# Attention softmax: one reciprocal for two heads, and sink logits that stay in a column of four buffers

## What is computed

```python
s = jnp.where(valid, s + alibi, -jnp.inf)
sink_logit = jnp.broadcast_to(sink.astype(jnp.float32).reshape(Hkv, rep, 1, 1), ...)
p = jax.nn.softmax(jnp.concatenate([s, sink_logit], axis=-1), axis=-1)[..., :-1]
o = jnp.einsum('bngrqk,bnkgd->bnqgrd', p, vb)
```

## Time and profile before

| what | value |
|---|---|
| median of three runs | 731.63 us (731.01 to 731.79) |
| the profiled execution | 729.93 us |
| its span in the profile | 728.1 us |
| TensorE busy | 703.9 us, 97% of the span |
| VectorE busy | 507.8 us, 70% |
| ScalarE busy | 389.6 us, 54% |
| GpSimd busy | 322.6 us, 44% |
| chain that ended last | TensorE 86%, DMA 5%, VectorE 4% |
| line 1544 (sink copies) | 16, 3.4 us in all |
| line 1554 in 140 to 270 us (reciprocals) | 93, 14.6 us in all |
| granted TensorE clock, mean | 0.995 |

### The profile page before, as it was taken

How to read it: one execution, slowest core, us unless ns; L and a number is a source line. 1 busy time by engine, 2 the same in 40 slices (tenths; PEclk the granted TensorE clock), 3 DMA queues, 4 the chain that set the end, 5 groups by cost and what they waited for, 6 DMA issues and landing times.

```text
span 728.1 us, 10269 instructions
## 1 busy us (share of the span) xinstructions
PE 703.9 (97%) x3761; PEld 510.4 (70%) x3761; DVE 507.8 (70%) x813; ACT 389.6 (54%) x586; POOL 322.6 (44%) x243
## 2 busy tenths in 40 slices
PE   7999999999999999999999999999999999999973
PEld 7888888886775556888888766666666666666631
DVE  5646422215988887214387998888888888888977
ACT  6500000104888887001122688888888888888815
POOL 2433458953778771610001444444444444442213
PEclk9999999999999999999999999999999999999998
DMA  9422112100500003705666599999999999999978
GB/s 308 141 59 59 32 56 59 30 0 22 124 1 2 1 1 136 211 2 203 230 224 227 180 370 387 388 386 384 383 385 382 390 386 383 383 386 380 392 267 345
DMA packets 62515, 158.06 MB, mean 217 GB/s; under 512 B 10184, under 2 KB 25008, under 8 KB 62464
## 3 DMA queue, kind: packets, MB, share of 16 engines
q1 hardware_dynamic: 55728, 139.58, 52.9%
q0 software_dynamic: 6432, 17.21, 7.0%
q10 hardware_dynamic: 304, 0.59, 0.2%
HBM read 142.69 MB, written 18.87 MB: 222 GB/s over the span
## 4 chain that ended last, share of the span: by engine, by line
PE 86%; DMA 5%; DVE 4%; SPq 1%; issue 1%; ACT 1%; POOL 0%; DVEq 0%; POOLq 0%
PE ps L1021 7%; PE ps L1028 7%; PE ps L1031 7%; PE ps L731 6%; PE ps L730 6%; PE ps L729 6%; PE ps L833 4%; PE ps L895 4%; PE ps L897 4%; PE ps L896 4%; PE ps L1054 4%; PE ps L1050 4%; PE ps L1058 4%; PE ps L818 3%; PE ps L857 3%; DMA wd<-in_expert_w_down 3%
## 5 line engine op out<-in xcount | busy, mean ns | idle before, releaser
L1833 DVE TENSOR_TENSOR wgulo<-wgu,unit 128x2048 fp32r<-128x2048 f32 x64 | 146.3, 2287 | 26.6 <-ACT unit L1291 26.6
L1291 ACT CAST unit<-wgu 128x2048 fp32r<-128x2048 f32 x64 | 122.2, 1909 | 1.8 <-DVE eid L1794 0.9
L2126 POOL DMA_INDIRECT expert_rows<-ysb,idx x32 | 71.5, 2236 | 106.7 <-ACT ysb L1344 97.3
L2119 POOL DMA_INDIRECT xg<-h_rows,idx x32 | 58.6, 1833 | 68.1 <-PE ps L990 58.6
L729 PE MATMUL ps<-hThi,whi 128*128 128x512 f32 x200 | 78.4, 392 | 0.0
L731 PE MATMUL ps<-hThi,wlo 128*128 128x512 f32 x200 | 78.0, 390 | 0.0
L730 PE MATMUL ps<-hTlo,whi 128*128 128x512 f32 x200 | 77.9, 390 | 0.0
L1839 DVE TENSOR_TENSOR wdlo<-wd,unit 128x2048 fp32r<-128x2048 f32 x32 | 73.1, 2285 | 2.3 <-ACT unit L1300 2.2
L1021 PE MATMUL ps<-unit,xThi 128*80 128x512 f32 x256 | 70.9, 398 | 0.2 <-ACT xThi L1312 0.2
L1028 PE MATMUL ps<-unit,xTlo 128*80 128x512 f32 x256 | 69.2, 392 | 0.0
L1031 PE MATMUL ps<-wgulo,xThi 128*80 128x512 f32 x256 | 69.2, 391 | 0.0
(11 more groups left out here) (231 smaller groups left out, 1448.9 us busy)
## 6 DMA issues: line engine op xcount, KB each, us to landing
wgu<-in_expert_w_gate SPq DMA_DIRECT2D x64, 512.0 KB, 11.8
wgu<-in_expert_w_up SPq DMA_DIRECT2D x64, 512.0 KB, 14.8
wd<-in_expert_w_down SPq DMA_DIRECT2D x32, 1024.0 KB, 17.0
y<-expert_rows SPq DMA_DIRECT2D x16, 512.0 KB, 10.6
wraw<-in_w_in SPq DMA_DIRECT2D x14, 512.0 KB, 3.8
xin<-in_x SPq DMA_DIRECT2D x8, 512.0 KB, 6.7
x<-in_x SPq DMA_DIRECT2D x8, 512.0 KB, 7.1
out<-fo SPq DMA_DIRECT2D x8, 512.0 KB, 3.9
```

What stands on the lines that cost most here:

```text
L1291: nc.scalar.copy(weight_unit(e, a)[:], raw_half(wgu, e, a)).then_inc(ahi_done, 1)
L1833: nc.vector.tensor_tensor(raw_half(wgulo, e, a), raw_half(wgu, e, a), weight_unit(e, a)[:].bitcast(F32), ALU.subtract).then_inc(alo_done, 1)
```

## The change

The reciprocals of two units are taken in one instruction of 128x2 at odd ticks only, for units u - 3 and u - 2, after the exponential of the later one. VectorE's own normalisations of both units follow it. For odd units the tick stays as it was; for even units reciprocal and normalisation move one tick back. In the sliding window the sinks lie in column 385 of the buffer, which has 386 columns now; the biased scores are written to the columns that end at 384, and the exponential reads the columns up to 385 and writes one column lower, so that the sinks stay. They are copied only in steps 8 to 11, once for each buffer; steps 12 to 23 have no copy and no wait for one.

```diff
--- before.py
+++ after.py
@@ -196,7 +196,7 @@
         qs = at("qs", [P, SWA_HEADS // 2, S], F32, Q + 16 * KB)
         oT = at("oT", [P, KT, S], F32, H)
         pna = [at(f"pna{i}", [P, 4, 3 * P], F32, H + 32 * KB + i * 6 * KB) for i in range(4)]
-        pswa = [at(f"pswa{i}", [P, 4, 3 * P + 1], F32, off) for i, off in enumerate((H + 56 * KB, TD + 8 * KB, TMP, Q + 8 * KB))]
+        pswa = [at(f"pswa{i}", [P, 4, 3 * P + 2], F32, off) for i, off in enumerate((H + 56 * KB, TD + 8 * KB, TMP, Q + 8 * KB))]
         ptna = [at(f"ptna{i}", [P, 5, 512], F32, W + 4 * KB + i * 10 * KB) for i in range(2)]
         ptswa = [[at(f"ptswa{i}_{c}", [P, 2, 512], F32, W + 4 * KB * (1 + 3 * i + c) if 3 * i + c < 5 else Q) for c in range(3)]
                  for i in range(2)]
@@ -435,7 +435,14 @@
             s = u // 4
             if s < NA_STEPS:
                 return pna[s % 4][:, u % 4, 0:steps[s][4]]
-            return pswa[s % 4][:, u % 4, 1:1 + steps[s][4]]
+            return pswa[s % 4][:, u % 4, 3 * P - steps[s][4]:3 * P]
+
+        def biased(u):
+
+            s = u // 4
+            if s < NA_STEPS:
+                return pbuf(u)
+            return pswa[s % 4][:, u % 4, 3 * P + 1 - steps[s][4]:3 * P + 1]
 
         def sbank(u):
             return u % 4
@@ -1185,11 +1192,12 @@
             def exponentials(u):
                 s = u // 4
                 act.wait_ge(bias_done, u + 1)
-                buf = pbuf(u)
+                probs, logits_ = pbuf(u), biased(u)
                 if s >= NA_STEPS:
 
-                    buf = pswa[s % 4][:, u % 4, 0:1 + steps[s][4]]
-                nc.scalar.activation(buf, buf, ACT.Exp, bias=mneg[:, u:u + 1], scale=-1.0,
+                    first = 3 * P - steps[s][4]
+                    probs, logits_ = pswa[s % 4][:, u % 4, first:3 * P + 1], pswa[s % 4][:, u % 4, first + 1:3 * P + 2]
+                nc.scalar.activation(probs, logits_, ACT.Exp, bias=mneg[:, u:u + 1], scale=-1.0,
                                      accum_out=esum[:, u:u + 1]).then_inc(exp_done, 1)
 
             def o_evacuate(s):
@@ -1533,7 +1541,7 @@
                     first = k0 // P - (i - 1)
                     tab = (ti if nk == 3 * P else te)[:, h, first * P:first * P + nk]
                     nc.vector.tensor_tensor_reduce(
-                        out=pbuf(u), in0=ps[:, sbank(u), 0:nk], in1=tab, scale=-(HD ** -0.5), scalar=BIG, op0=ALU.add, op1=ALU.min,
+                        out=biased(u), in0=ps[:, sbank(u), 0:nk], in1=tab, scale=-(HD ** -0.5), scalar=BIG, op0=ALU.add, op1=ALU.min,
                         accum_out=mneg[:, u:u + 1]).then_inc(bias_done, 1)
                 else:
                     hh = 4 * g + h
@@ -1541,17 +1549,23 @@
 
                         if s >= NA_STEPS + 4:
                             dve.wait_ge(tr_done, chunk_no[(s - 4, last_chunk[s - 4])] + 1)
-                        nc.vector.tensor_copy(pswa[s % 4][:, :, 0], nsink[:, 4 * g:4 * g + 4]).then_inc(sink_set, 1)
-                        dve.wait_ge(sink_set, 2 + s - NA_STEPS)
+                        else:
+                            nc.vector.tensor_copy(pswa[s % 4][:, :, 3 * P + 1], nsink[:, 4 * g:4 * g + 4]).then_inc(sink_set, 1)
+                            dve.wait_ge(sink_set, 2 + s - NA_STEPS)
                     first = (k0 // P) - (i - 1)
                     nc.vector.tensor_tensor_reduce(
-                        out=pbuf(u), in0=ps[:, sbank(u), 0:nk], in1=dist[:, first * P:first * P + nk],
+                        out=biased(u), in0=ps[:, sbank(u), 0:nk], in1=dist[:, first * P:first * P + nk],
                         scale=SLOPES[hh], scalar=nsink[:, hh:hh + 1], op0=ALU.add, op1=ALU.min,
                         accum_out=mneg[:, u:u + 1]).then_inc(bias_done, 1)
 
-            def reciprocal(u):
-                dve.wait_ge(exp_done, u + 1)
-                nc.vector.reciprocal(esum[:, u:u + 1], esum[:, u:u + 1]).then_inc(recip_done, 1)
+            def reciprocals(u):
+
+                dve.wait_ge(exp_done, u + 2)
+                nc.vector.reciprocal(esum[:, u:u + 2], esum[:, u:u + 2]).then_inc(recip_done, 2)
+
+            def normalised(u):
+                dve.wait_ge(recip_done, u + 1)
+                nc.vector.tensor_scalar(pbuf(u), pbuf(u), esum[:, u:u + 1], None, ALU.mult).then_inc(norm_v, 1)
 
             def wo_split(k):
 
@@ -1564,11 +1578,11 @@
             for u, tick in enumerate(ticks):
                 if u < NU:
                     bias_and_max(u)
-                if 0 <= u - 2 < NU:
-                    reciprocal(u - 2)
-                    if norm_by_vector(u - 2):
-                        dve.wait_ge(recip_done, u - 1)
-                        nc.vector.tensor_scalar(pbuf(u - 2), pbuf(u - 2), esum[:, u - 2:u - 1], None, ALU.mult).then_inc(norm_v, 1)
+                if 0 <= u - 3 < NU and u % 2 == 1:
+                    reciprocals(u - 3)
+                for x in (u - 3, u - 2) if u % 2 == 1 else ():
+                    if 0 <= x < NU and norm_by_vector(x):
+                        normalised(x)
                 if u in LAST_QUERIES:
                     projected(2 * MT - 2 + LAST_QUERIES.index(u))
                 if u == NU + POOL_LAG:
```

## The result

Twelve runs each: the changed kernel 732.0 us median (730.83 to 733.41), the kernel before 730.7 us (729.29 to 731.82). The ratio is 1.0017, 95% interval 1.0009 to 1.0025: slower by 1.2 us by the ratio, less than 0.2%, and clear of noise. The profiled execution has a span of 730.4 us.

What follows compares the result with a forecast made beforehand. TensorE was taken as the bound, VectorE counting only where TensorE waits for it. Terms 1.05 + 0 + 0.2 - 0.4 - 0.3 = + 0.55 us on 731.63 gave 732.2 us, range 730.0 to 734.6.

Steps and rivals of the forecast that it cites:

- The evacuation is not ready: Even step, after the first bias: VectorE's evacuation waits for transposes until 2.19 us behind the scores, idling about 0.6 us.
- 0.35 us for each repeating pair: Three sliding-window pairs of steps: the moved normalisation ends the odd step's scores 0.35 us later each, + 1.05 in all.
- L: Distance from the start of an even step's scores to its fourth bias's read-out; forecast to grow from 4.56 to 4.91 us.
- The pair at 225.04: nothing: Pair of steps starting at 225.04 us: the distance was already 4.94 us and would be 4.91, so change 0.
- The last pair: + 0.2: Last pair of steps, with 256 keys: estimated at about half of the full pair's 0.35 us, + 0.2.
- GpSimd gets its units no later than needed, the pairing adds no wait that counts: GpSimd's runs begin with odd units, whose tick stays; at odd ticks VectorE already waited for the same exponential.
- The unknown price, 0.33: Moved normalisation beside GpSimd's first one: taken to hold VectorE's queue 0.33 us, with 0.62 kept as the alternative.
- The rivals of a stall: Moved normalisation stalls beside GpSimd, 733.9 us, chance 0.18; or GpSimd takes the ports first, 738 us, chance 0.04.
- The step of - 0.4: Pair before the one at 225.04, where VectorE never waits: removed instructions count there, a gain of 0.4 us.
- The step of - 0.3: Two neighbourhood steps before the score group at 183.37: VectorE taken as the bound, four reciprocals less gain 0.3 us.
- the moved normalisations stretch nothing in the neighbourhood steps: Later neighbourhood steps: assumed that normalisations moved there (units 14, 22, 30) stretch no score group.
- The slack that the prediction couldn't size: Neighbourhood steps: unstretched score groups have their biases in time, by how much their length doesn't say.

Runs made afterwards that it cites:

- e4: Kernel before, but in the sliding window VectorE normalises unit 5 of every eight instead of unit 6; 730.90 us, ratio 1.0003 to the kernel before.
- e3: Changed kernel, but in the sliding window VectorE normalises unit 5 of every eight instead of unit 6; 729.07 us, ratio 0.9979 to the kernel before.
- e6: Changed kernel with the reciprocal pairs taken at even ticks, so unit 6 is normalised where it was before; 729.55 us, ratio 0.9986 to the kernel before.
- e2: Kernel before with the paired reciprocals alone, sink copies and old columns kept; 732.25 us, ratio 1.0026 to the kernel before.
- e5: Changed kernel, but in the sliding window VectorE evacuates a step's first chunk of transposes and ScalarE the second; 727.10 us, ratio 0.9950 to the kernel before.
- e12: Kernel before with paired reciprocals, sink copies kept, and VectorE evacuating the first chunk of a step; 729.38 us, ratio 0.9979 to the kernel before.
- e1: Changed kernel with the single reciprocals and order of before, so only the sinks that stay; 730.51 us, ratio 0.9999 to the kernel before.
- e9: Kernel before (single reciprocals, sink copies) with VectorE evacuating the first chunk of a step; 730.33 us, ratio 0.9992 to the kernel before.
- e11: Kernel before with the sinks that stay, single reciprocals, and VectorE evacuating the first chunk of a step; 726.99 us, ratio 0.9946 to the kernel before.
- e8: Changed kernel, but in the sliding window the moved normalisation is issued one bias later, behind the third; 731.47 us, ratio 1.0012 to the kernel before.
- e7: Changed kernel with VectorE evacuating the first chunk in the sliding window and normalising unit 5 instead of 6 in all steps; 726.92 us, ratio 0.9944.

## Why the prediction was right, and where it was off

Right, step by step:
- *The evacuation is not ready*: 0.61 us of idle time stands there, 0.6 was given, and e4 shows the shadow in the kernel before.
- *0.35 us for each repeating pair*: 0.37 to 0.38 was measured, 1.14 for the three against 1.05. L 4.93 for 4.91. The 0.02 is the distance from the fourth bias to its read-out, 0.54 (249.64 to 250.18), where 0.52 had been read; every start before it is within 0.01 of the one worked out.
- *The pair at 225.04: nothing*: 9.81 before, 9.82 after. *The last pair: + 0.2*: from its start to the output projection + 0.23.
- *GpSimd gets its units no later than needed, the pairing adds no wait that counts*: e3 and e6.
- *The unknown price, 0.33*: the normalisation took 0.42 and held the queue for 0.34. The rivals of a stall did not happen to the moved instruction.

Off were the two gains. The sum had - 0.3 and - 0.4 and came to + 0.55; measured were - 0.14 and - 0.03, and + 1.20. So the change was over twice the forecast one, and that 732.2 stands so near the measured 732.0 us is in good part luck: the forecast started from the 731.63 us of three runs, and twelve runs of the kernel before gave 730.7. The two errors nearly cancel.

The step of - 0.4 was that the pair ahead of 225.04 gains what is removed. Its own part was right: 3.25 us from evacuation to read-out were given and 3.26 measured (218.35 to 221.61). But the evacuation started 0.75 us behind the scores at 217.60, where before it was 0.42 (217.41 against 216.99). The timeline of VectorE after, and of before, for the step ahead of it:

```profile
214.86 0.35 DVE L1553 COPY pswa<-nsink 128x4 f32<-128x4 f32 x1 [0.35 <-PE ps L825]
...
216.52 0.76 DVE L1568 TENSOR_SCALAR pswa<-pswa,esum 128x384 f32<-128x384 f32 x1
...
218.35 0.66 DVE L501 COPY ptswa<-ps 128x512 f32<-128x512 f32 x1
```

```profile
214.25 0.17 DVE L1544 COPY pswa<-nsink 128x4 f32<-128x4 f32 x1 [0.43 <-PE ps L818]
...
215.79 0.49 DVE L1571 TENSOR_SCALAR pswa<-pswa,esum 128x384 f32<-128x384 f32 x1
```

The timelines of GpSimd after, and of before, for the instructions that these two start inside:

```profile
214.61 1.24 POOL L2087 TENSOR_SCALAR pswa<-pswa,esum 128x384 f32<-128x384 f32 x1 [0.46 <-DVE esum L1564]
...
215.83 1.24 POOL L2087 TENSOR_SCALAR pswa<-pswa,esum 128x384 f32<-128x384 f32 x1
```

```profile
213.61 1.25 POOL L2073 TENSOR_SCALAR pswa<-pswa,esum 128x384 f32<-128x384 f32 x1
...
214.83 1.24 POOL L2073 TENSOR_SCALAR pswa<-pswa,esum 128x384 f32<-128x384 f32 x1
```

The sink copy takes 0.35 us instead of 0.17, the normalisation of unit 43 0.76 instead of 0.49. In both kernels they run beside GpSimd, and after the change they meet its instructions at another moment: the copy starts 0.25 us into one instead of 0.64, the normalisation 0.69 instead of 0.96. That this is the cause is shown by the other traces: the copy took 0.34 or 0.35 us wherever it started at 0.25 or 0.26 (e2, e5, e12) and 0.17 at 0.63 or 0.64 (e1, e9, e11); the normalisation took 0.76 or 0.77 at 0.69 (e2, e3, e6, e8) and 0.49 or 0.50 at 0.96 (e1, e7). I had costed collisions with GpSimd for the moved instruction alone.

The step of - 0.3 held at first: the group that answers to the one at 183.37 is 2.17 long, and A's running difference was - 0.25 one group later. Then the assumption failed that the moved normalisations stretch nothing in the neighbourhood steps:

```profile
184.00 2.17 PE L820 MATMUL ps<-ka,qa 64*128 64x384 f32 x8
...
188.74 1.67 PE L820 MATMUL ps<-ka,qa 64*128 64x384 f32 x8
```

The second group is 1.67 long, 0.11 more than before, and e7, where unit 5 takes unit 6's place, has 1.56 there. The slack that the prediction couldn't size was smaller than the move. Whether - 0.3 would have come without it is not shown: in e6, where unit 6 is back at its old tick, that group is 1.56 long too, yet the group behind it starts 26.15 us after the first scores, as after the change (before: 26.29). The odd units' normalisations move in e6, so it is no clean test of this.

## What to carry to other kernels

Before an instruction is counted as a saving, find what the engine waits for next: what was taken off VectorE's queue in a repeating pair became idle time, 0.61 us in front of the evacuation and 2.32 instead of 1.67 in front of the even step's scores. An instruction that moves across such a wait, from the shadow into the path, costs all the time for which it holds the queue (here 0.34 us, and about 0.1 of waiting for its reciprocal), even if it was moved in order to save others. Work through one period of the loop as a chain of starts; here that gave each wait to some hundredths, while the one-off stretches, where two engines meet at a changing moment, did not follow.

## What the runs showed of the hardware

- The two normalisations that start almost together, in the timelines of VectorE and of GpSimd after (the last row is GpSimd's whole run of six):

```profile
238.96 0.42 DVE L1568 TENSOR_SCALAR pswa<-pswa,esum 128x384 f32<-128x384 f32 x1
```

```profile
239.02 1.47 POOL L2087 TENSOR_SCALAR pswa<-pswa,esum 128x384 f32<-128x384 f32 x1 [2.09 <-DVE esum L1564]
239.02 7.73 POOL L2087 TENSOR_SCALAR pswa<-pswa,esum 128x384 f32<-128x384 f32 x6 [2.09 <-DVE esum L1564]
```

GpSimd's first instruction starts 0.06 us after VectorE's (238.96) and takes 1.47 us instead of 1.24; VectorE's keeps its 0.42. The Trainium skill, "SBUF — State Buffer", section "Who interferes with whom", says that the first to start has the shared ports for its whole instruction and that the other blocks fully. The order is as this pair has it, but not the amount: GpSimd loses 0.23 us where 0.36 of VectorE's instruction were left.
- Where GpSimd is first, it matters how far into its instruction VectorE's starts. In all fourteen traces, by the profile's spans, which are rough for GpSimd, and for normalisations of 128x384 on both engines (GpSimd's is 1.24 us):

| VectorE's starts, us into GpSimd's | VectorE's normalisation of 128x384 | count |
|---|---|---|
| 0.06 to 0.35 | ends 0.79 or 0.80 us after GpSimd's start (takes 0.74 down to 0.44 us) | 36 |
| 0.37 to 0.66 | takes 0.42 us; from 0.48 on GpSimd's takes longer, up to 1.43 us | 61 |
| 0.69 to 1.03 | ends 0.21 or 0.22 us after GpSimd's end (takes 0.77 down to 0.42 us) | 67 |

By that rule VectorE would wait for GpSimd's end in all three rows; the traces agree in the last one alone. The instructions at 216.52 above (0.76 us) and at 241.66 in the earlier trace rows (0.70) belong to it. That none of the twelve in the earlier trace rows was over 0.45 us, which the prediction held against a stall, is due to their starts: the seven of 128x384 that start inside a GpSimd instruction do so 0.35 to 0.48 or 1.02 us into it. In e6 and e7, where they start at other moments, the neighbourhood steps have normalisations of 0.73 us.
- A reciprocal of 128x2 takes the same 0.16 us, and the same 0.07 to 0.08 of the queue, as one of 128x1.
- A copy of 128x4 takes 0.16 or 0.17 us alone. Inside a GpSimd normalisation of 128x384 it ends 0.60 us after GpSimd's start where it starts 0.09 to 0.42 us into it (0.50 down to 0.18 us; one copy in e4 ended at 0.70), takes 0.16 to 0.18 where it starts at 0.43 to 0.64, and ends 0.02 or 0.03 us after GpSimd's end where it starts at 0.73 to 0.99 (0.54 down to 0.28 us).
